# Swapped halves of nineteen rotations by transfers within on-chip memory instead of permutation products, in a kernel of two transformer blocks

## The reference

```
def apply_rope(x, cos, sin):
    d2 = x.shape[-1] // 2
    x1, x2 = x[..., :d2], x[..., d2:]
    return concatenate([x1 * c - x2 * s, x1 * s + x2 * c], axis=-1)
```

## Time and profile before

| | |
|---|---|
| median of 3 runs | 1343.58 us (1343.05 to 1343.72) |
| span of the profiled execution | 1346.5 us |
| PE busy | 1310.0 us (97%) |
| DVE, ACT, POOL busy | 822.6, 630.6, 94.4 us |
| mean granted clock of TensorE | 0.978 |

### The profile page before, as it was taken

One profiled execution on the slowest core, in us unless ns is written; L12 is line 12 of the kernel. 1 busy time (PEld: TensorE's weight loads), 2 busy tenths in 40 slices (PEclk: granted clock), 3 DMA queues, 4 the chain that ended last, 5 costly groups with the idle time before them and its releaser, 6 DMA issues.

```text
span 1346.5 us, 21653 instructions
## 1 busy us (share of the span) xinstructions
PE 1310.0 (97%) x8900; PEld 1192.0 (89%) x8900; DVE 822.6 (61%) x951; ACT 630.6 (47%) x843; POOL 94.4 (7%) x73
## 2 busy tenths in 40 slices
PE   8999999999989999999999999999999999999997
PEld 7999999789978999999988789999998878899996
DVE  4655556566556555556688656555567976655554
ACT  5444445476524544445744445444464334644443
POOL 0000001100000000000441100000004220000000
PEclk9999999899799999999999899999998989999999
DMA  8565566453125465556524235555643332465551
GB/s 270 187 219 186 184 158 177 126 157 91 67 95 185 155 209 187 187 187 181 157 85 143 64 125 188 188 188 186 181 150 119 107 104 80 156 200 187 186 192 46
DMA packets 173540, 209.94 MB, mean 156 GB/s; under 512 B 24232, under 2 KB 149792, under 8 KB 173344
## 3 DMA queue, kind: packets, MB, share of 16 engines
q1 hardware_dynamic: 173024, 208.52, 49.2%
q10 hardware_dynamic: 448, 0.46, 0.2%
HBM read 207.92 MB, written 1.05 MB: 155 GB/s over the span
## 4 chain that ended last, share of the span: by engine, by line
PE 88%; DVE 4%; ACT 2%; issue 2%; SPq 1%; POOL 1%; DMA 1%; DVEq 0%; POOLq 0%; ACTq 0%
PE bank L1778 70%; PE bank L2221 4%; PE bank L2104 3%; PE bank L2083 3%; PE bank L1855 2%; PE bank L2026 1%; DVE w_lo L1288 1%; PE bank L2090 1%; ACT w_hi L937 1%; POOL scr L863 1%; DMA raw<-in_ffn_up_dram 1%; PE bank L2138 1%; PE bank L2077 1%; PE bank L1835 1%; SPq L769 1%
## 5 line engine op out<-in xcount | busy, mean ns | idle before, releaser
L1288 DVE TENSOR_TENSOR w_lo<-raw,w_hi 128x2048 fp32r<-128x2048 f32 (+2 forms) x198 | 444.7, 2247 | 297.9 <-ACT w_hi L937 297.4
L937 ACT ACTIVATE w_hi<-raw 128x2048 fp32r<-128x2048 f32 (+2 forms) x198 | 367.7, 1861 | 243.0 <-PE bank L1778 222.4
L1778 PE MATMUL bank<-n_hi,w_hi 128*128 128x256 f32 x1664 | 476.8, 287 | 4.7 <-DVE w_lo L1288 2.8
L1778 PE MATMUL bank<-n_lo,w_hi 128*128 128x256 f32 x1664 | 473.0, 284 | 0.0
L1778 PE MATMUL bank<-n_hi,w_lo 128*128 128x256 f32 x1664 | 472.9, 284 | 0.0
L1778 PEld LDWEIGHTS bank<-n_hi,w_hi 128*128 128x128 f32 x1664 | 320.2, 192 | 10.6 <-issue 4.7
L1778 PEld LDWEIGHTS bank<-n_lo,w_hi 128*128 128x128 f32 x1664 | 320.2, 192 | 2.3 <-issue 0.5
L1778 PEld LDWEIGHTS bank<-n_hi,w_lo 128*128 128x128 f32 x1664 | 319.9, 192 | 0.0
L1778 PE MATMUL bank<-w_hi,hid_hi 128*128 128x512 f32 (+1 forms) x472 | 182.3, 386 | 1.8 <-DVE hid_lo L1361 1.1
L1778 PE MATMUL bank<-w_lo,hid_hi 128*128 128x512 f32 (+1 forms) x472 | 181.6, 385 | 0.0
L1778 PE MATMUL bank<-w_hi,hid_lo 128*128 128x512 f32 (+1 forms) x472 | 181.1, 384 | 0.0
(11 more groups left out here) (256 smaller groups left out, 1572.0 us busy)
## 6 DMA issues: line engine op xcount, KB each, us to landing
raw<-in_w_ff_dram SPq DMA_DIRECT2D x64, 1024.0 KB, 5.2
raw<-in_w_in_dram SPq DMA_DIRECT2D x31, 1024.0 KB, 5.3
raw<-in_ffn_down_dram SPq DMA_DIRECT2D x22, 1024.0 KB, 4.9
raw<-in_ffn_up_dram SPq DMA_DIRECT2D x21, 1024.0 KB, 5.3
raw<-in_ffn_gate_dram SPq DMA_DIRECT2D x20, 1024.0 KB, 5.3
raw<-in_w_out_dram SPq DMA_DIRECT2D x12, 1024.0 KB, 5.1
raw<-in_w_uq_dram SPq DMA_DIRECT2D x8, 576.0 KB, 4.0
raw<-in_w_in_dram SPq DMA_DIRECT2D x12, 256.0 KB, 4.1
```

The costliest lines, as they stand in the source:

```text
L937: nc.scalar.activation(w_hi[:, s % SPLIT, c0:n], raw[:, s % RING, c0:n], ACT.Copy).then_inc(hi_ready, 1)
L1288: V.tensor_tensor(w_lo[:, s % SPLIT, c0:n], raw[:, s % RING, c0:n], w_hi[:, s % SPLIT, c0:n].bitcast(f32), ALU.subtract).then_inc(lo_ready, 1)
L1778: mm = MM(out, stat(k, a), mov(k, b), start=(first and k == 0 and n == 0), stop=(last and k == K - 1 and n == 2), skip_group_check=True)
```

## The change

For nineteen of the 29 rotations (`k`, `nq0`, `nq1`, `sq0`, `sq1` in layer 0; `aq`, `rk`, `rq`, `uq0` to `uq3` in layers 1 and 2) TensorE's product goes. Behind its copy into `xs`, ACT waits for that copy and issues transfers from `xs` to a new buffer `xr` that exchange blocks of 32 partitions (four transfers of 64 KB each) or, for `uq`, of 16 partitions (two of 32 KB). DVE waits for their semaphore and multiplies `xr`, not the bank, by a table of sines that now has the signs. The other permutation matrices lose their signs. The banks of the later products are dealt out anew, since nineteen jobs take none.

To make room for `xr`, the constants `band` and `cmp_mask` go to scratch by a transfer of their own; `g_ret_2` is no longer loaded at the start but in layer 1, behind the second table, into `gret`, whose place the tables of the positions take till then; and the operand of the warm-up products is 128 columns wide and read four times over.

```diff
-CONST1 = [..., ("causal", 256), ("band", 256), ("cmp_mask", 256), ("cmp_vis", 256), ("cos_a", 256), ("sin_a", 256)]
+CONST1 = [..., ("causal", 256), ("cmp_vis", 256), ("cos_a", 256), ("sin_a", 256), ("band", 256), ("cmp_mask", 256)]
...
-            if (c // half) % 2 == 0:
-                m[c + half, c] = -1.0
-            else:
-                m[c - half, c] = 1.0
+            m[c + half if (c // half) % 2 == 0 else c - half, c] = 1.0
...
+SWAPPED = {"nq0": 32, "nq1": 32, "sq0": 32, "sq1": 32, "k": 32, "aq": 32, "rk": 32, "rq": 32,
+           "uq0": 16, "uq1": 16, "uq2": 16, "uq3": 16}
...
-                for l in range(2):
-                    sp.dma_start(gret[:, l, :], A["g_ret_2"][l:l + 1, :].to_broadcast([P, T])).then_inc(small_in, 16)
...
-                sp.dma_start(cst[:, P:NC1], const1[:, P:NC1]).then_inc(consts_in, 16)
+                sp.dma_start(cst[:, P:KEPT1], const1[:, P:KEPT1]).then_inc(consts_in, 16)
+                sp.dma_start(band_in, const1[:, KEPT1:NC1]).then_inc(band_there, 16)
...
                         sp.dma_start(tables, const2).then_inc(tables_in, 16)
+                        for l in range(2):
+                            sp.dma_start(gret[:, l, :], A["g_ret_2"][l:l + 1, :].to_broadcast([P, T])).then_inc(gret_in, 16)
...
+            def swap(st, name, buf):
+
+                act.wait_ge(*free_count(st))
+                half = SWAPPED[name]
+                for p in range(64, MLA_Q, half) if name.startswith("uq") else range(0, P, half):
+                    q = p + half if (p // half) % 2 == 0 else p - half
+                    act.dma_start(xr[p:p + half, buf, :], xs[q:q + half, buf, :]).then_inc(swap_in[buf], 16)
...
                         nc.scalar.activation(xs[:, buf, :], pb[:, :], ACT.Copy, scale=scale).then_inc(freed(st), 1)
+                        if name in SWAPPED or name == "kk":
+                            swap(st, "k" if name == "kk" else name, buf)
...
-                    pb = await_bank(dve, st)
+                    if st[2] in SWAPPED:
+                        buf = XSC[st[1:]][1]
+                        dve.wait_ge(swap_in[buf], SWAPS[st[1:]])
+                        pb = xr[:, buf, :]
+                    else:
+                        pb = await_bank(dve, st)
...
-                    V.tensor_tensor(view[0], view[1], s_, ALU.mult).then_inc(freed(st), 1)
-                    dve.wait_ge(*free_count(st))
+                    ins = V.tensor_tensor(view[0], view[1], s_, ALU.mult)
+                    if st[2] in SWAPPED:
+                        link(ins)
+                    else:
+                        ins.then_inc(freed(st), 1)
+                        dve.wait_ge(*free_count(st))
...
-                elif kind == "rope":
+                elif kind == "rope" and st[2] not in SWAPPED:
```

More of the change, by code:

```diff
@@ L66 @@
 C1, NC1 = columns(CONST1)
+KEPT1 = C1["band"][0]
 C2, NC2 = columns(CONST2)
@@ L99, in constants, with signs @@
     rows = np.arange(P)
-    put("inv64", inv(32)[rows % 32][:, None])
+    def signs(half):
+        return np.where((rows // half) % 2 == 0, -1.0, 1.0)[:, None]
+    put("inv64", (inv(32)[rows % 32][:, None] * signs(32)).astype(np.float32))
     put("blk", (rows[:, None] // CP == np.arange(8)[None, :]).astype(np.float32))
@@ L110, in constants @@
     put("cos_a", np.cos(angles(32, rows)))
-    put("sin_a", np.sin(angles(32, rows)))
+    put("sin_a", signs(32) * np.sin(angles(32, rows)))
     put("cos_i", np.cos(angles(16, rows)))
-    put("sin_i", np.sin(angles(16, rows)))
+    put("sin_i", signs(16) * np.sin(angles(16, rows)))
     turned = (rows >= 64)[:, None]
     put("cos_m", np.where(turned, np.cos(angles(16, rows)), 1.0))
-    put("sin_m", np.where(turned, np.sin(angles(16, rows)), 0.0))
+    put("sin_m", np.where(turned, signs(16) * np.sin(angles(16, rows)), 0.0))
     gamma = np.log1p(-np.exp2(-5.0 - np.arange(4)))
@@ L243, in two_blocks @@
         xs1 = sb("xs1", [P, 1, T])
+        xr = sb("xr", [P, 2, 512])
         turn_c, turn_s = sb("turn_c", [P, 2, 512]), sb("turn_s", [P, 512])
@@ L276, in two_blocks @@
         tables = scr[:, 2048:4096]
+        band_in = scr[:, 2048:2560]
         nqT, sqT = region(4096, 4, T), region(5120, 4, T)
@@ L331, in two_blocks @@
         ident_in, gain0_in, x_in = sem("ident_in"), sem("gain0_in"), sem("x_in")
-        consts_in, pos_in, small_in = sem("consts_in"), sem("pos_in"), sem("small_in")
+        consts_in, pos_in, small_in, band_there = sem("consts_in"), sem("pos_in"), sem("small_in"), sem("band_there")
         setup = sem("setup")
         pool_setup = sem("pool_setup")
-        trig, tables_in = sem("trig"), sem("tables_in")
+        trig, tables_in, gret_in = sem("trig"), sem("tables_in"), sem("gret_in")
+        swap_in = [sem(f"swap_in{i}") for i in range(2)]
         h_ready = sem("h_ready")
@@ L402, in two_blocks @@
         XSC, RO, BUFUSE = {}, {}, {}
+        SWAPS, _swaps = {}, [0, 0]
         ATT, PVN, ON = {}, {}, {}
@@ L500, in two_blocks @@
                 RO[st[1:]] = len(RO)
-                job(st)
+                if st[2] in SWAPPED:
+                    buf = XSC[st[1:]][1]
+                    _swaps[buf] += 128 // SWAPPED[st[2]] if not st[2].startswith("uq") else 2
+                    SWAPS[st[1:]] = 16 * _swaps[buf]
+                else:
+                    job(st)
             elif kind == "cmp1":
@@ L1172, in _ @@
                     nc.scalar.activation(xs[0:MLA_Q, buf, :], pb[0:MLA_Q, :], ACT.Copy, scale=MLA_Q ** -0.5).then_inc(freed(st), 1)
+                    swap(st, f"uq{n}", buf)
                 elif kind == "ukv":
@@ L1888, in keep_warm @@
                 for _ in range(n):
-                    MM(bank[7][:, :], zerob[:, 0:P], zerob[:, :], start=True, stop=True, skip_group_check=True)
+                    MM(bank[7][:, :].rearrange("p (a c) -> p a c", a=4), zerob[:, :], zerob[:, :].unsqueeze(1).to_broadcast([P, 4, P]), start=True,
+                       stop=True, skip_group_check=True)
             def turn_gains(st):
```

27 lines of the change are left out of this document (15 added, 12 removed).

## The result

| | before | changed |
|---|---|---|
| median | 1342.16 us (20 runs, 1339.95 to 1345.84) | 1344.72 us (20 runs, 1343.20 to 1345.88) |
| ratio | | 1.0014 (95% interval 1.0008 to 1.0020), +1.9 us |
| PE busy | 1310.0 us | 1290.8 us |
| DVE, ACT, POOL busy | 822.6, 630.6, 94.4 us | 826.9, 630.5, 90.7 us |

The forecast was 1344.0 and no change that can be told; the time came out 0.14% longer. The profiled execution of before (span 1346.5) was a long one: in every execution of the changed kernel the span was 1.8 us less than the time, so this one's own time was about 1348.3 (an estimate), not the 1346.5 that the prediction took.

What follows compares the result with a forecast made beforehand. TensorE held 88% of the chain of waits; of 16.5 us taken from it nearly all is given back by VectorE and ScalarE. Terms sum to +0.4 us, span 1346.9, median 1344.0; range 1337.5 to 1348.5.

Steps and rivals of the forecast that it cites:

- Start: First chain's wait for a slab behind the constants: 256 KB of `g_ret_2` leave that queue, -0.8 us.
- Issues on ScalarE: Four transfer issues per rotation hold ScalarE 1.9 us; layer 1's rank norms, behind aq's copy, start 1.5 us later.
- Landing: Transfers' arrival between copy and use: nothing counted even at 6.4 us, though sq1's addition must wait.
- VectorE's product with sin waits for GpSimd: Both operands in SBUF: 0.85 us at sq0, 1.1 at nq1, 0.8 at aq, 0.85 at rk, none at uq1.
- Layer 0: Product at k goes, 1.8 us earlier; GpSimd costs +1.0 on `xpe`, +0.85 at sq0, 1.1 at nq1: +1.2 us.
- Clock: TensorE pauses longer before layer 0's scores, whose stretch runs mostly at 1.2 GHz: +0.4 us.
- Given back at 724: VectorE operation of 1.37 us under GpSimd's uq1 product falls to about 0.3: -1.1 us in each of layers 1 and 2.
- Layers 1 and 2: Layer 1 +0.8 us, layer 2 -1.2 with rounding, each after ScalarE's waits of 0.34 and 0.65 take up 1.0.
- the first (no wait for GpSimd): Rival: VectorE's product with sin does not wait for GpSimd; 7.6 us fall away, 1336.4 us; chance 0.24.
- TensorE binding throughout: Rival: TensorE binds everywhere, so all 16.5 us and the start's 0.8 are gained: 1326.3 us; chance 0.04.
- The third: Rival: ScalarE's issues take 1.0 us each while SyncE's transfers are queued, in all three layers: +6.6, 1350.6 us; chance 0.14.
- The fourth, a longer half-rate stretch: Rival: TensorE waits more before all three layers' scores, half-rate stretches growing, 1.5 us a layer: 1348.5 us; chance 0.06.

Runs made afterwards that it cites:

- the start alone: Changed kernel's loading of constants, late `g_ret_2`, narrow warm-up operand and signed sine tables, all rotations keeping TensorE's product: ratio 0.9987 to the kernel before, -1.7 us.
- the balance: Start alone against the changed kernel without transfers and with GpSimd's product cut short: nineteen products worth 8.5 us; GpSimd takes back 6.0, transfers 6.0: +3.5.

## Why the prediction was right, and where it was not

The forecast and the range held, in part by luck, since errors of opposite sign stand in the sum: the start came out 0.9 us better than forecast (more by the profiles), layer 0 2.0 us worse.

- *Start: -0.8.* Measured -1.7 (-3.0 to -0.5), and 3 us in every profile. The sign is right; the size was read from the 256 KB alone. Which of the changes to the start gives the rest was not tried.
- *Issues on ScalarE: 0.45 us each, four in 1.9.* They take 0.61 (median of 60), four in 2.5. The rank norms of layer 1 are 55.41 - 53.12 = 2.3 us later, where 1.5 were forecast; the VectorE instruction ahead of them waits 4.18 us for idx 1's copy.
- *Issues in layer 0: no term.* This is what the sum left out. The prediction says of k's issues that they are not hidden, but puts no price on them. The transfers put off layer 0's first score by 2.0 us; k's issues hold up the rounding that VectorE's next split awaits, and issued later they give back 0.8.
- *Landing: nothing.* In the changed kernel this held, although the landings were slow: beside the loads of the compression weights they took up to 5.6 us (median 4.5 of the 20 in layer 0). At sq0 the landing ended just as the split did (247.47 against 247.44). At sq1 VectorE stood 2.29 us. The sign that I had named for being wrong, scores that stand for sq1's landing, did not come: TensorE does not wait between the first score and 300 us, and without any transfer it takes no less from the first transposes to the next addition (154.06 against 154.05). In layers 1 and 2 the landings have a median of 2.2 us. The Trainium skill, page "DMA: Bandwidth & Descriptors", section "Anatomy of one DMA — SWDGE (gpsimd) path", has some 2.0 us of fixed cost for a transfer that GpSimd issues. These are ScalarE's; the least of 60 here is 1.9 and the median 2.4, which is near it, and in layer 0 the median was more than twice that.
- *VectorE's product with sin waits for GpSimd: 5.3 us in all.* Right in kind, shown by changing the operand alone: 3.9 us. It showed at sq0, nq1 and aq as forecast, not at rk (GpSimd had ended at 697.47, since the split came later), but also at uq1, where I had counted no loss. The Trainium skill, page "SBUF — State Buffer", section "Who interferes with whom", gives the same rule, and this case agrees: 0.69 us with one operand in a bank, up to 1.78 with both in SBUF.
- *Layer 0: +1.2 until the first score product.* From the split to that product it is 58.44 us against 57.06: +1.4. The number is right, its parts are not. By the table, against the start alone, the products of TensorE gone and GpSimd out of the way give 3.7 (54.99 - 51.29) where I had 1.8, though these 3.7 hold what GpSimd did before too; GpSimd takes 3.1 where I had 2.95; the transfers take 2.0 where I had nothing.
- *Clock: +0.4.* Too small, by some 0.8 as the profiles have it: 1.2 between the means of two and six executions, which scatter by 1.5 among themselves. The forecast pause of 6 us was 7.95. By the times layer 0 costs 3.6 (give or take 1.5) instead of 1.6; the profiles account for 1.4 before the first score and 1.2 after it.
- *Given back at 724: -1.1 a layer; ScalarE's waits: -1.0.* Both seen: 0.29 us for the operation, and the root of the retention's norm follows the exponentials without a wait.
- *Layers 1 and 2: -0.4 together.* Measured 0 (give or take 1.5).

Of the four rivals, the first (no wait for GpSimd) is refuted by the operand experiment, and TensorE binding throughout by the balance. The third put a loss on issues of 1 us; at 0.61 each lies between my 0.45 and its point of decision, 0.7. What it said of their place was right for layer 0, where they stand in the path. The fourth, a longer half-rate stretch, shows in layer 0 (1.2 us beside a scatter of 1.5, where I had put 0.4), and was not seen to grow in layers 1 and 2 (from 744 to 757 us the changed kernel runs at a granted 1.00, where in before two products took 3.47 us).

What stays open: the 1 us or so of layer 0's 3.6 that the profiles do not find (it is within the scatter), what a filled pause would be worth without sq1's landing, and whether aq, rk and uq1 are worth exchanging once aq's issues are out of the way.

## What to carry to other kernels

Before taking work from the busiest engine, ask what the replacement reads and from where: moving one operand from a bank to SBUF made VectorE wait for GpSimd, and that alone cost 3.9 us. Issue a transfer from a compute engine's queue behind that engine's longer work, not straight behind the small copy it depends on; the same 60 transfers then cost 3.2 us less. Put a price on every place where issues stand ahead of other work; in layer 0 the transfers, which had none, put off the first score by 2.0 us. Such a change need not be made everywhere: nine of nineteen, chosen by the timelines, made the kernel 0.4% faster where all nineteen made it 0.14% slower (the new start, 0.13%, is in both).

## What the runs showed of the hardware

- An issue of ScalarE runs beside its own running activation (673.04 to 674.18 and 673.17 to 674.35 overlap), and its median is 0.61 us whether it moves 64 KB or, cut in two, 32 KB.
- TensorE's granted clock fell to 0.50 within a pause of 7.95 us, before there was work again, and stayed at 1.00 when the pause was filled with products into a bank that is overwritten. The same work behind a pause of 2.4 us took 13.05 us in one execution of the kernel before and 14.57 in another, both in part at 0.50. That is 1.5 of the 4.3 us by which their spans differ, and may be behind some of its scatter, 1340 to 1346 us.
- Transfers of 64 KB within SBUF landed 4.5 us after their issue in layer 0, beside the loads of the compression weights (median of 20), and 2.0 us in layers 1 and 2 (median of 24).
